# Hybrid mixer of a two-block fp32 network: convolution on VectorE alone, other PSUM banks, later SiLU, weight halves ahead of the centring

## What is computed

```python
def second_block(x, ...):
    for l in range(2):
        x = layer_norm(alpha * x + 0.5 * swiglu_2(x, w_ff1_in[l], w_ff1_out[l]), ln1_g[l], ln1_b[l])
        mix = hybrid_mixer(x, ...)
        x = layer_norm(alpha * x + mix, ln2_g[l], ln2_b[l])
        x = layer_norm(alpha * x + 0.5 * swiglu_2(x, w_ff2_in[l], w_ff2_out[l]), ln3_g[l], ln3_b[l])

def hybrid_mixer(x, w_in, b_in, ...):
    (qa, ka, va, beta_raw, a_raw, za, qb, kb, vb, qc, kc, vc) = jnp.split(x @ w_in + b_in, split_at, axis=-1)
    o_a = gated_deltanet(qa, ka, va, beta_raw, a_raw, za, ...)   # causal depthwise convolution of 4 taps on
                                                                 # q, k, v, SiLU, l2 norm of q and k, delta rule
    o_b = chunk_relpos_attention(qb, kb, vb, rel_bias)           # 4 heads of 128
    o_c = swa_sink_attention(qc, kc, vc, sinks)                  # 8 heads of 64, 2 of keys, a sink
    gates = sigmoid(x @ w_gate + b_gate).reshape(b, t, 3, d)
    merged = gates[:, :, 0] * (o_a @ w_br_a) + gates[:, :, 1] * (o_b @ w_br_b) + gates[:, :, 2] * (o_c @ w_br_c)
    return merged @ w_out
```

## Time and profile before

| | |
|---|---|
| median of 3 runs | 2555.53 us (2553.45 to 2555.55) |
| the profiled execution | 2554.28 us, span 2552.2 us |
| PE busy | 2431.1 us (95%) |
| DVE busy | 1801.2 us (71%) |
| ACT busy | 1304.5 us (51%) |
| POOL busy | 115.7 us (5%) |
| granted TensorE clock, mean | 0.974 |

### The profile page before, as it was taken

The page is one execution under the profiler, slowest core; times in us unless marked ns, Lnnn a source line. Parts: engine busy times, 40 slices in busy tenths (PEclk is TensorE's granted clock), DMA queues, the critical chain, the costliest instruction groups (busy, mean ns, idle before and its releaser), DMA issues.

```text
span 2552.2 us, 39046 instructions
## 1 busy us (share of the span) xinstructions
PE 2431.1 (95%) x15856; PEld 2221.0 (87%) x15856; DVE 1801.2 (71%) x2679; ACT 1304.5 (51%) x1995; POOL 115.7 (5%) x104
## 2 busy tenths in 40 slices
PE   7789999989999999889998999999998899989998
PEld 7678889887888888889998888898888899988887
DVE  4659757567867876777467876688767664678864
ACT  5545454545544544556454554455445663545543
POOL 0002100001200000210000000000002100000000
PEclk9899999999999999999999999999999899999999
DMA  5236565344656565533253656556664332446652
GB/s 182 83 112 213 180 209 181 129 133 144 191 185 198 190 187 185 179 122 108 92 164 126 206 185 187 166 187 198 186 187 160 112 111 97 158 134 204 188 175 91
DMA packets 114882, 409.92 MB, mean 161 GB/s; under 512 B 12816, under 2 KB 14992, under 8 KB 114704
## 3 DMA queue, kind: packets, MB, share of 16 engines
q1 hardware_dynamic: 114704, 407.43, 49.9%
HBM read 406.33 MB, written 1.05 MB: 160 GB/s over the span
## 4 chain that ended last, share of the span: by engine, by line
PE 86%; DVE 9%; ACT 4%; issue 1%; DMA 0%; SPq 0%; ACTq 0%; DVEq 0%
PE ps L359 85%; DVE wlo L1655 3%; ACT whi L1007 1%; ACT region L1170 1%; PE ps L568 0%; DVE x L1812 0%; DVE x L1830 0%; DVE region L1855 0%; DVE xx L1710 0%; DVE region L1950 0%; DMA cst<-in_consts 0%; DVE region L2226 0%; DVE region L2184 0%; DVE region L2312 0%; DVE region L2223 0%
## 5 line engine op out<-in xcount | busy, mean ns | idle before, releaser
L359 PE MATMUL ps<-xx,whi 128*128 128x256 f32 (+1 forms) x4912 | 1346.9, 345 | 40.5 <-ACT region L1404 16.1
L1655 DVE TENSOR_TENSOR wlo<-raw,whi 128x1024 fp32r<-128x1024 f32 (+3 forms) x772 | 935.6, 1217 | 444.5 <-ACT whi L1007 442.9
L1007 ACT ACTIVATE whi<-raw 128x1024 fp32r<-128x1024 f32 (+3 forms) x772 | 800.7, 1043 | 531.4 <-PE ps L359 531.0
L359 PE MATMUL ps<-xx,wlo 128*128 128x256 f32 x3688 | 1046.3, 284 | 0.0
L359 PEld LDWEIGHTS ps<-xx,whi 128*128 128x128 f32 x4912 | 864.8, 193 | 156.5 <-ACT region L1404 16.5
L359 PEld LDWEIGHTS ps<-xx,wlo 128*128 128x128 f32 x3688 | 709.9, 192 | 0.3
L359 PE MATMUL ps<-H,whi 128*128 128x512 f32 (+1 forms) x2400 | 686.7, 351 | 22.1 <-DVE wlo L1655 10.4
L359 PE MATMUL ps<-H,wlo 128*128 128x256 f32 x1888 | 534.7, 283 | 0.0
L359 PEld LDWEIGHTS ps<-H,whi 128*128 128x128 f32 x2400 | 425.5, 191 | 86.4 <-issue 14.6
L359 PEld LDWEIGHTS ps<-H,wlo 128*128 128x128 f32 x1888 | 358.9, 190 | 0.2
L1650 DVE TENSOR_REDUCE t<-ps 128x256 f32<-128x512 f32 x308 | 211.7, 689 | 51.5 <-PE ps L359 42.4
(11 more groups left out here) (271 smaller groups left out, 1564.0 us busy)
## 6 DMA issues: line engine op xcount, KB each, us to landing
raw<-in_sg SPq DMA_DIRECT2D x128, 512.0 KB, 3.8
raw<-in_su SPq DMA_DIRECT2D x128, 512.0 KB, 3.5
raw<-in_sd SPq DMA_DIRECT2D x128, 512.0 KB, 3.9
raw<-in_mw_g SPq DMA_DIRECT2D x48, 512.0 KB, 3.5
raw<-in_fg SPq DMA_DIRECT2D x44, 512.0 KB, 3.4
raw<-in_fu SPq DMA_DIRECT2D x44, 512.0 KB, 3.6
raw<-in_fd SPq DMA_DIRECT2D x32, 512.0 KB, 3.5
raw<-in_mw_a SPq DMA_DIRECT2D x24, 512.0 KB, 3.8
```

Of the source, the lines that this page charges most:

```text
L359: return e.matmul(out, lhsT, rhs, start=start, stop=stop, skip_group_check=True)
L1007: e.activation(m.whi[:, c % NHL, 0:cw], m.raw[:, c % NRAW, 0:cw], ACT.Copy).then_inc(s["whi"].h, s["whi"].up(c))
L1655: e.tensor_tensor(m.wlo[:, c % NHL, 0:cw], m.raw[:, c % NRAW, 0:cw], m.whi[:, c % NHL, 0:cw].bitcast(F32), ALU.subtract).then_inc(s["wlo"] ...
```

## The change

Six edits, all in the hybrid mixer, in both layers, and in `attend`, which it calls.

1. DVE does all three later taps of the convolution, each waiting for the one before it. POOL's part is gone; it only copies the identity matrices, now once tile mw_a7 is done.
2. The query and key tiles mw_c0 to c4 go to banks 0, 1, 2, 3, 0 instead of 0, 1, 0, 1, 0. ACT and DVE take the convolution's inputs 4 to 7 between these tiles instead of ahead of them. The scaled bias of the queries is computed first on DVE. The conv blocks are spread otherwise over DVE's tiles.
3. `attend` has a `yield` ahead of its second four heads, and the number of steps between scores and normalisation is (3, 2) for C and 3 for B instead of 2.
4. ACT's SiLU of all six pairs stands after mw_qkb2, and `delta` is added there on all engines; the cast of a mask on DVE (layer 0 only) goes one tile later.
5. The output tiles go to banks 2, 3, 4, 5, 0, 1, 6, 7 instead of 0 to 7, the centring's matmul to bank 1 instead of 0.
6. The halves of mw_o5, o6 and o7 stand ahead of the centring on ACT and DVE instead of behind it.

```diff
 def tensor_program(e, m):
-    def attend(tag, nh, qf, kf, vf, S, PT, bks, put, ready, vready=(), gap=2):
+    def attend(tag, nh, qf, kf, vf, S, PT, bks, put, ready, vready=(), gaps=(2,)):
         for h0 in range(0, nh, 4):
+            if h0:
+                yield
...
-            for _ in range(gap):
+            for _ in range(gaps[h0 // 4]):
                 yield
...
-            gemm_fm(f"mw_c{l}", i, take(i % 2, ("pact", l, "c", i))[:, 0:256], xh, xl)
+            gemm_fm(f"mw_c{l}", i, take(i % 4, ("pact", l, "c", i))[:, 0:256], xh, xl)
...
-            if i == 1:
+            if i == 2:
                 side.add(delta())
...
-        gemm_first(f"g{l}", [(f"mw_o{l}", n, take(n, ("xadd", st, n))[:, 0:256]) for n in range(3)], a=m.mx)
+        gemm_first(f"g{l}", [(f"mw_o{l}", n, take(m.mo_bank[n], ("xadd", st, n))[:, 0:256]) for n in range(3)], a=m.mx)
...
             if n == 3:
-                centre(st, 0)
+                centre(st, 1)
 def scalar_program(e, m):
-        for i in range(6):
-            if i < 4:
-                produce(1, 4)
+        def raw(i):
             w.wait_ge(s["rawn"], l, i)
             e.activation(m.pr[i], m.pr[i], ACT.Identity, scale=-1.0, bias=m.wgb[:, i, 1:2]).then_inc(
                 s["pact"].h, s["pact"].up(l, "a", i))
             tap(i)
-        for i in range(6, 8):
+
+        for i in range(4):
+            produce(1, 4)
+            raw(i)
+        for _ in range(2):
             chunk()
-            taps(i)
         for i in range(5):
             chunk()
             w.wait_ge(s["gemm"], f"mw_c{l}", i)
...
             t.then_inc(s["pact"].h, s["pact"].up(l, "c", i))
+            if i < 2:
+                raw(4 + i)
+            elif i < 4:
+                taps(4 + i)
...
         for i in range(8, 12):
             chunk()
             taps(i)
-            if i == 11:
-                for p in range(5):
-                    conv(p)
             side.step()
...
-            if i == 1:
-                conv(5)
+            if i == 2:
+                for p in range(6):
+                    conv(p)
                 side.add(delta())
...
         for n in range(2, 8):
-            if n >= 3:
+            if n < 7:
                 chunk()
             if n == 2:
                 w.wait_ge(s["xlo"], f"g{l}", 7)
-            norm_tile(f"t{l}", (f"l2g{l}", f"l2b{l}"), n, 3, 0)
+            norm_tile(f"t{l}", (f"l2g{l}", f"l2b{l}"), n, 3, 1)
 def vector_program(e, m):
         def conv(i):
+
             y, pr = m.cv[:, i, :], m.pr[i]
-            w.wait_ge(s["cpool"], l, i)
-            e.scalar_tensor_tensor(y[:, 2:256], pr[:, 0:254], pk(f"cw{l}", 12 + i), y[:, 2:256], ALU.mult,
-                                   ALU.add).then_inc(s["cdve"].h, s["cdve"].up(l, "2", i))
-            w.wait_ge(s["cdve"], l, "2", i)
-            e.scalar_tensor_tensor(y[:, 3:256], pr[:, 0:253], pk(f"cw{l}", i), y[:, 3:256], ALU.mult,
-                                   ALU.add).then_inc(s["cdve"].h, s["cdve"].up(l, i))
+            w.wait_ge(s["pact"], l, "a3", i)
+            for d in (1, 2, 3):
+                e.scalar_tensor_tensor(y[:, d:256], pr[:, 0:256 - d], pk(f"cw{l}", 12 * (3 - d) + i), y[:, d:256], ALU.mult,
+                                       ALU.add).then_inc(s["cdve"].h, s["cdve"].up(l, d, i))
+                w.wait_ge(s["cdve"], l, d, i)
...
         for i in range(5):
             chunk()
-            if i:
-                conv(i - 1)
+            if i < 2:
+                raw(m.pr[4 + i], ps[4 + i], 4 + i, ((f"mw_a{l}", 4 + i), (l, 4 + i)), pk(f"bqa{l}", 4 + i))
+            else:
+                conv(i - 2)
...
-            if i in (0, 1, 2, 4):
-                conv(4 + i if i < 4 else 7)
+            if i % 2 == 0:
+                conv(3 + i // 2)
             side.step()
...
-            if i > 8:
-                conv(i - 1)
+            conv(i - 2)
             side.step()
...
-            if i == 0:
-                conv(11)
-            if i == 1:
+            if i < 2:
+                conv(10 + i)
+            if i == 2:
                 side.add(delta())
-            if i == 2 and l == 0:
+            if i == 3 and l == 0:
...
         for n in range(8):
-            norm_tile(f"t{l}", (f"l2g{l}", f"l2b{l}"), n, 3, add_one, (f"mw_o{l}", n), n)
-            if n >= 3:
+            if n == 2:
+                chunk()
+            norm_tile(f"t{l}", (f"l2g{l}", f"l2b{l}"), n, 3, add_one, (f"mw_o{l}", n), m.mo_bank[n])
+            if 3 <= n < 7:
                 chunk()
 def gpsimd_program(e, m):
-        for i in range(12):
...
-            w.wait_ge(s["pact"], l, "a", i)
...
-            e.tensor_scalar(r, pr, pk(f"cw{l}", 24 + i), None, ALU.mult).then_inc(s["cpool"].h, s["cpool"].up(l, "r", i))
...
-            e.tensor_tensor(y[:, 1:256], y[:, 1:256], r[:, 0:255], ALU.add).then_inc(s["cpool"].h, s["cpool"].up(l, i))
-        w.wait_ge(s["cpool"], l, 11)
+        w.wait_ge(s["gemm"], f"mw_a{l}", 7)
```

More of the change, by code:

```diff
@@ L256, in lay_memory @@
         m.sm[:, 2 * i:2 * i + 2, :] for i in range(11))
-    wide = [v.rearrange("p (a b) c -> p a (b c)", b=2) for v in (m.AT, m.kbg, m.T)]
+    wide = [v.rearrange("p (a b) c -> p a (b c)", b=2) for v in (m.AT, m.kbg)]
     m.pr = [v[:, i, :] for v in (m.pre, wide[0], wide[1]) for i in range(4)]
-    m.tap = [wide[2][:, i, :] for i in range(2)]
+    m.mo_bank = [2, 3, 4, 5, 0, 1, 6, 7]
     m.bq8 = m.rowc[:, ROWC:ROWC + 4]
@@ L763, in both @@
                               lambda h: [m.vb[:, n, h * 128:h * 128 + 128] for n in range(2)], m.S, m.S, [2, 3], put_b,
-                              [("pact", l, "qk", 7)])
+                              [("pact", l, "qk", 7)], gaps=(3,))
             flag.add("B")
@@ L1155, in ffn, with attend @@
             tile(n)
-    def attend(tag, nh, S, PT, st, bks, sink, put, gap=2):
+    def attend(tag, nh, S, PT, st, bks, sink, put, gaps=(2,)):
         for h0 in range(0, nh, 4):
+            if h0:
+                yield
             yield
@@ L1171, in attend @@
                                  accum_out=st[:, 2, c:c + 1]).then_inc(s["aact"].h, s["aact"].up("e", tag, h0 + i, g))
-            for _ in range(gap - 1):
+            for _ in range(gaps[h0 // 4] - 1):
                 yield
@@ L1421, in both @@
         def both():
-            yield from attend(("c", l), 8, m.S, m.S, m.st, [2, 3], True, put_c)
+            yield from attend(("c", l), 8, m.S, m.S, m.st, [2, 3], True, put_c, gaps=(3, 2))
             flag.add("C")
@@ L1425, in both @@
                 yield
-            yield from attend(("b", l), 4, m.S, m.S, m.st, [2, 3], False, put_b)
+            yield from attend(("b", l), 4, m.S, m.S, m.st, [2, 3], False, put_b, gaps=(3,))
             flag.add("B")
@@ L1931, in ffn, with attend @@
             tile(n, (wd, (n + 1) * down_chunks(nt) - 1))
-    def attend(tag, nh, bias, S, st, bks, put, scale, sink=None, slope=None, gap=2):
+    def attend(tag, nh, bias, S, st, bks, put, scale, sink=None, slope=None, gaps=(2,)):
         for h0 in range(0, nh, 4):
+            if h0:
+                yield
             for i in range(4):
```

31 lines of the change are left out of this document (12 added, 19 removed).

## The result

The changed kernel takes 2564.86 us (median of 7 runs, 2560.79 to 2565.88), the kernel before 2555.53 in the same comparison: a ratio of 1.003, with a 95% interval of 1.0016 to 1.0045. It is slower, where I forecast 2549 and a range up to 2559.

What follows compares the result with a forecast made beforehand. PE, busy 2431.1 of 2552.2 us, was taken as the bound. With low clock, -1.4 - 1.0 + 2 x 3.8 = 5.2 us gained against 2554.28 gave 2549.1; forecast 2549, range 2530 to 2559.

Steps and rivals of the forecast that it cites:

- D: PE's 0.57 us wait at 1152.80 for DVE's reciprocal root of the norms; forecast to end at about 1155.3.
- All four times: Forecast layer 0 times: key tile 1081.5, transposes 1109.4, decay matmuls 1130.3, root of the norms 1155.3.
- A: PE's 8.06 us wait at 1075.17 for a query tile's eviction; forecast replaced by some 3 us for the key tile.
- C: PE's 2.25 us wait at 1129.96, ahead of the decay matmuls; forecast replaced there by a wait of 4.4 us.
- the two cancel: Convolution: the third tap's +6 us of DVE a layer against 5 to 6 back from POOL's contention; DVE's sum unchanged.
- The clock at D: Behind the wait for the root of the norms, nearer 3 us, a low-clock stretch was to cost 1.7 us.
- Each time at or behind a wait of 2.25 us or more: Where PE's clock is low in layer 0 before the change; not behind the 1.57 us wait.
- From 1156 to 1340 ... nothing in the likeliest case: Attention steps against gemm tiles, PE always busy: no gain possible, two to six us of margin, likeliest loss nothing.
- My own sign of being wrong: The forecast would be wrong if D came before 1152 with the extra tile done, or PE waited before the output projection.
- the front: Mixer up to D: 1.4 us lost in layer 0 and 1.0 in layer 1, low clock included.
- The output projection: Waits of 1.57 and 5.20 us go, 1.2 and 2.2 come: 5.5 us gained a layer, 3.8 with low clock.
- The slower rival: D costs 3 us more and the margin to 1340 is used up: 2556 to 2563, chance 0.14.

Runs made afterwards that it cites:

- pool_tap_back: The changed kernel with edits 1 and 4 undone, so POOL does convolution tap 1 again and SiLU and the delta step stand where they were: 2543.89 us.
- changed_pool_tap_back: The changed kernel with edit 1 alone undone, so POOL does convolution tap 1 again: 2558.19 us.
- squares_ahead: The changed kernel with the two squares of the output norm one step earlier on ACT, ahead of the gate's eviction: 2553.5 us.
- only_output_halves: The kernel before with edits 5 and 6 alone: 2547.79 us.

## Why the prediction was wrong, step by step

- *Up to D: right.* All four times came within half a microsecond, partly by luck: the terms named add up to 1108.8 at the transposes and 1154.8 at D, and the last 0.6 and 0.5 us of the forecasts were put on without a row. The mechanism held, the transposes, the decay matmuls and D being set by DVE as worked out. That A and C go and come back as other waits was right, and so was the extra weight of the three-op convolution being covered at DVE's sum; that it costs nothing was not. It costs 6 us in the new order, by the runs without it (pool_tap_back, changed_pool_tap_back). It was in my chain, and so in D's time; my sentence "the two cancel" only hid it.
- *The clock at D: mis-sized.* I took 1.7 us for a stretch of 3.5; it lasted 6.9 of which PE worked 5.85, 2.9 lost, and 2.1 in layer 1. I also took the rows of before for more regular than they are. "Each time at or behind a wait of 2.25 us or more" leaves out a low stretch of before from 1144.57 on, 14 us behind PE's last wait (C), and "layer 1 has the same waits" leaves out that C is 1.96 us there, with a low stretch behind it. Windows of the kernel before, as in the earlier trace rows:

```profile
1144.57:1151.40 6.83, 6.83 (x34) 6.83 (x34) 2.39 (x6) 5.53 (x20) 0.00 (x0) 0.50 0.15 42
...
2018.38:2021.80 3.42, 3.42 (x19) 3.42 (x18) 3.32 (x8) 0.00 (x0) 0.00 (x0) 0.50 0.46 153
```

- *"From 1156 to 1340 ... nothing in the likeliest case": the step that failed.* I looked at how much each engine had in hand there and took the moved generators as moved alike on all engines. They are moved alike against tiles, but the tiles aren't alike: from the gates on they come in threes, and ACT's gate eviction stands in one of the three. By one tile the squares went from in front of it to behind it. The order on ACT showed that, at a place from which I gave no piece. Its price, 2 us of wait and 3.4 of low clock a layer, is what squares_ahead gives back (11.4 us), and with it the change comes out level with before. My own sign of being wrong, a PE wait between D and the output projection, came true three times a layer.
- *The 16 us between forecast and result*: the squares 2 x 5.4 = 10.8, the two small waits of 0.8 in each layer 3.2, the front with its low clock 5.8 lost instead of 2.4, less 1.7 that the output projection gave beyond its 7.6.
- *The output projection: right*, 8 us by the run of it alone, for a forecast of 3.8 with and 5.5 without the low clock behind the two waits. By the marks it is 4.3 and 5.0 with it, and 5.8 and 6.3 without it in only_output_halves.
- *The slower rival* had the mark (D later than 1161, or the stretch to 1340 used up) on D. D came at 1155.65; the loss was behind it, by a mechanism that no rival named. My chance of 0.11 for slower was too low for a stretch of 184 us that I had not worked through.

## What to carry to other kernels

Where side work is woven between tiles by step counts, moving it by one step changes its phase against the tiles; look at each wait of the critical engine for what stands in the same queue just ahead of its releaser, and put work whose input is ready in front of an eviction that waits for a tile. A PE wait of 2 us cost 5.4 in the changed kernel and 3.7 in changed_pool_tap_back, so short waits are worth removing one by one. Test the parts of a bundle alone: edits 5 and 6 gave 8 us, and with edits 2 and 3, without 1 and 4, 11.
